# A feed-forward block with seven-product pairs: its start reordered, and one weight sum of each pair made by an accumulating DMA

## The chip, the cores and the metric

The kernel runs on one core of a Trainium2 chip. The metric is the device time of one execution in microseconds (us); lower is better. Everything below is read from one profiled execution of the kernel before the change.

## The reference, cut to what matters

The program computes two small transformer stacks for 256 tokens (two tiles of 128) of width 1024, all in 32-bit floats. The part that the change touches is the gated feed-forward of the first stack. It is computed four times: before and after the mixer, in each of two layers.

```python
D_MODEL, SEQ, D_FF = 1024, 256, 2816

def _swiglu(x, w1, w3, w2):
    return (jax.nn.silu(x @ w1) * (x @ w3)) @ w2

for l in range(DEPTH):                       # DEPTH = 2
    h = _swiglu(x, ffn_w1[l, 0], ffn_w3[l, 0], ffn_w2[l, 0])
    x = _layernorm(ALPHA * x + 0.5 * h, ln_g[l, 0], ln_b[l, 0])
    h = _mixer(x, l, ...)
    x = _layernorm(ALPHA * x + h, ln_g[l, 1], ln_b[l, 1])
    h = _swiglu(x, ffn_w1[l, 1], ffn_w3[l, 1], ffn_w2[l, 1])
    x = _layernorm(ALPHA * x + 0.5 * h, ln_g[l, 2], ln_b[l, 2])
# then the second stack (attention variants, squared-ReLU feed-forward), not touched
```

## The kernel before, in words

**Split products.** Every 32-bit product is made of three passes of a reduced form of float: a weight tile is split into a high part, which ScalarE writes by a cast (`w_high`), and a low part, which VectorE writes as raw minus high (`w_low`). TensorE then runs high by high, high by low and low by high. So each 1 MB weight unit (128 x 2048 values) costs ScalarE a cast, VectorE a subtraction, and TensorE 24 matmuls of 128 x 512 in a plain unit or 12 in a summed one.

**Ring of four slots.** The raw, high and low tiles have four slots. SyncE (SP) loads units in a fixed order; each load waits until VectorE has read the slot's former raw content (semaphore `slot_lo`). ScalarE waits until TensorE has used the slot's former high part (`unit_used`).

**One feed-forward.** The 2816 hidden columns are eleven blocks of 256. Five are plain (`h0`, `h1`, `h4`, `h7`, `h10`): two units each for the up products (`h1_0` is block 1, first half of K) and one for the down product (`d0`). The other six go in three pairs (`q` = 0, 1, 2) of the seven-product form, of which the kernel needs, for each pair, seven units made of four raw weight quarters R11, R21 (of w1), R12, R22 (of w3), each 128 x 2048. These stand in `sum_raw`, in the trace `buf_v` (R11), `buf_q` (R21), `buf_u` (R12) and `buf_val` (R22). The units are `b11` = R11 and `b21` = R21, then `v` = R11+R12, `x` = that plus R22, `w` = R12+R22, `y` = the sum in R11 plus R21, and `b22` = R22. `v`, `x` and `y` are made one after the other in the same tile R11, which can be overwritten only when the cast and the subtraction of the unit before have read it. `w` is made by an accumulating DMA that GpSimd issues (L705, semaphore `w_sum`); `v`, `x` and `y` are VectorE additions (`add_to`, L2671, semaphore `sum_done`). The left operands are four combinations of the quarters of x, the forms (`combine` L2704, cast to high L1974, low L2708), made once in each feed-forward.

**Order.** All engines run orders written out by hand, each in its own function: `ffn1` of SyncE, TensorE, ScalarE and VectorE. TensorE runs, in a pair, b11, b21, v, x, first half of a down product, w, second half, y, b22. Bank 1 of `aux` collects b11, then x, then w, then y, and ScalarE copies it out between them (`term1` after b11, `term2` after x, `term3` after w; L1997, L2006, L2010; `mix_param` in the trace). So TensorE starts `x` only after the term1 copy, `w` only after the term2 copy and `y` only after the term3 copy (semaphore `quad_act`).

**Start of a feed-forward.** TensorE runs block 0, block 1, the transposes of block 0's result (`plain_T(0)`), and then the down product d0, for which it needs the low part of that transposed result (`plain_low_T(0)`, L2681, `yT_low`). The down products collect in `acc`.

**End.** TensorE interleaves the last hidden block with the last down products (`last_T(t)` transposes block 10's result for token tile t; `last_low(t)`, L2694, is its low part); VectorE adds the result to x, takes the statistics and scales tile 0, then tile 1 (L2536 to L2585), while TensorE transposes the new x for the next stage (`x_T`, L842).

The cores of the functions follow, with the line numbers of the profile.

Of the kernel before, what the change touches and what calls it, by code (L numbers as in the profile page):

```python
# [48 lines left out]

def quad_and_plain(q, a, b):  # L50

    o = 3 * q + 4
    units = [(f"b11_{q}", a), (f"b21_{q}", b), (f"v_{q}", 1), (f"x_{q}", 2), (f"d{o - 3}", a), (f"w_{q}", b),
             (f"y_{q}", 1), (f"b22_{q}", 2), (f"h{o}_0", b), (f"h{o}_1", a), (f"d{o - 2}", 1), (f"d{o - 1}", 2)]
    done = [f"b11_{q}", f"b21_{q}", f"v_{q}", f"x_{q}", f"w_{q}", f"d{o - 3}", f"y_{q}", f"b22_{q}",
            f"h{o}_0", f"d{o - 2}", f"d{o - 1}"]
    return units, done


def ffn_units():  # L60

    order = [("h0_0", 0), ("h0_1", 1), ("h1_0", 3), ("h1_1", 1), ("d0", 2)]
    done = ["h0_0", "h1_0", "d0"]
    for q in range(QUADS):
        units, ends = quad_and_plain(q, *((3, 0) if q % 2 else (0, 3)))
        order += units
        done += ends
    order.append(("d10", 3))
    uses, loads, last_load, table = [0] * RING, [0] * RING, [None] * RING, {}
    for name, s in order:  # L70
        loaded = name[0] in "hd"
        table[name] = (s, uses[s], loads[s], last_load[s])
# [162 lines left out]
def build(nc, a, out, stop=None):  # L235
    ctx = ExitStack()
    with ctx:
# [67 lines left out]
        FORM_AT = (1, 2, 0, 3)  # L305
# [34 lines left out]
        w_sum = sem("w_sum")  # L340
        form_done = sem("form_done")
# [147 lines left out]
        def _(sp):  # L489
# [57 lines left out]
            def ffn1(l, which):  # L547
# [12 lines left out]
                for q in range(QUADS):  # L560
                    o = 3 * q + 4
                    down1(l, which, o - 3)
                    hidden1(l, which, o, 0)
                    down1(l, which, o - 2)
                    down1(l, which, o - 1)
# [90 lines left out]
        def _(pool):  # L656
# [42 lines left out]
            def sums_by_dma(l, which):  # L699

                for q in range(QUADS):
                    n = quads_before(l, which, q)
                    pool.wait_ge(sum_done, 3 * n + 1)
                    pool.wait_ge(r_full[R22], 16 * n + 16)
                    pool.dma_start(sum_raw[R12], sum_raw[R22], accum_op=ALU.add).then_inc(w_sum, 16)  # L705

# [98 lines left out]
        def _(pe):  # L805
# [196 lines left out]
            def ffn1(l, which, next_tile0):  # L1002
# [111 lines left out]
                def quad1(q):  # L1114
# [10 lines left out]
                    quad_product("x", q, 1, *form(1), False)  # L1125
                    plain_down(o - 3, 0)
                    pe.wait_ge(quad_act, terms + 2)
                    quad_product("w", q, 1, *form(2), False)
# [50 lines left out]
                quad_down(i - 2, 0)  # L1179
                quad_down(i - 1, 0)  # L1180
                last_T(0)
# [647 lines left out]
        def _(act):  # L1829
# [92 lines left out]
            def ffn1(l, which, tile1, next_tile0, mid):  # L1922
# [17 lines left out]
                def summed(q, n):  # L1940
                    act.wait_ge(sum_done, 3 * quads_before(l, which, q) + n)
# [24 lines left out]
                high_plain("h1_0")  # L1966
                high_plain("d0")
                activate(0, 1)
                high_plain("h1_1")
                loaded(0, R11)  # L1970
                high_sum("b11", 0, R11)
                for n in range(FORMS):
                    act.wait_ge(form_done, FORMS * (2 * l + which) + (1, 3, 2, 4)[n])
# [16 lines left out]
                for q in range(QUADS):  # L1990
# [11 lines left out]
                    summed(q, 3)  # L2002
# [15 lines left out]
                    high_plain(f"d{o - 2}")  # L2018
                    used(f"b22_{q}")
                    high_plain(f"d{o - 1}")  # L2020
# [6 lines left out]
                    high_sum("b11", q + 1, R11)  # L2027
                    activate(o, 1)
# [460 lines left out]
        def _(dve):  # L2489
# [165 lines left out]
            def ffn1(l, which, tile1, k_norm, next_tile0, mid, half_first):  # L2655
# [61 lines left out]
                multiply(0, 0)  # L2717
                whole(0, 0, 2)
                low_plain("h1_0")
# [5 lines left out]
                multiply(0, 1)  # L2725
                combine(2, 1, 2, ALU.subtract)
                dve.drain()
                combine(3, 3, 2, ALU.add)
                low_plain("h1_1")
# [4 lines left out]
                if mid is not None:  # L2734
                    mid()
                add_to(0, R11, R12)
                low_sum("b21", 0, R21)
                dve.wait_ge(aux_full[2], n_aux[2].k + 1)
                multiply(1, 0)
                plain_low_T(0)  # L2740
                multiply(1, 1)
                for q in range(QUADS):
# [7 lines left out]
                    add_to(q, R11, R21)  # L2750
# [13 lines left out]
                    low_plain(f"d{o - 2}")  # L2764
# [4 lines left out]
                    low_plain(f"d{o - 1}")  # L2769
                    multiply(o, 0)  # L2770
                    quad_low_T(q)
                    if q + 1 == QUADS:
                        break
                    low_sum("b11", q + 1, R11)
# [15 lines left out]
                if half_first:  # L2790
# [202 lines left out]
            def position_angles():  # L2993

                dve.wait_ge(angle_in, 2 * 16)
# [23 lines left out]
                dve.drain().then_inc(angles, 1)  # L3019
                dve.wait_ge(sines, 1)  # L3020
# [545 lines left out]
```

## Time and profile before

| what | value |
|---|---|
| median of 3 runs | 1984.37 us (1981.62 to 1985.58) |
| the profiled execution | 1983.09 us, its span 1981.1 us |
| TensorE busy | 1904.8 us, 96% of the span |
| VectorE busy | 1406.5 us, 71% |
| ScalarE busy | 1001.0 us, 51% |
| mean granted TensorE clock | 0.99 of full |
| the DMA engines, share of the span on the SP queue / GpSimd's queue | 48.9% / 6.0% |

The four feed-forwards of the first stack span about 0 to 212, 455 to 655, 655 to 850 and 1095 to 1300 us. TensorE is nearly always busy, so what counts is where it waits, and for what, and at which clock it runs behind the wait. A row of the timeline with "[6.08 <-DVE yT_low L2681]" says that the engine sat idle 6.08 us before this instruction and that VectorE's instruction of line 2681 ended the idle time. Durations of two instructions in a row overlap a little: subtractions of 2.28 us start 2.20 us apart.

### The profile page before, as it was taken

How to read it: one execution, taken by the hardware profiler on the slowest of the kernel's cores; microseconds unless marked ns; L12 is line 12 of the kernel's file. 1: busy time of each engine (PE TensorE's matmuls, PEld its weight loads, DVE VectorE, ACT ScalarE, POOL GpSimd, SP SyncE). 2: the span in 40 equal slices, each digit the busy share in tenths (PEclk: the TensorE clock that was granted, in tenths of full speed). 3: DMA queues.
4: the chain of work that ended last, by engine and by line, in shares of the span. 5: the costliest groups of instructions: out<-in, count | busy, mean ns of one | idle time of the engine just before them, and what ended most of it. 6: DMA issues, size and time to landing. Idle time of an engine off the chain costs nothing.

```text
span 1981.1 us, 23187 instructions
## 1 busy us (share of the span) xinstructions
PE 1904.8 (96%) x9016; PEld 1559.3 (79%) x9016; DVE 1406.5 (71%) x1599; ACT 1001.0 (51%) x1203; POOL 107.6 (5%) x176
## 2 busy tenths in 40 slices
PE   6999999999899899999999899989999999999999
PEld 5788788887788678878888678878788887778887
DVE  5788776678788878777667878778665567675545
ACT  4555435554455445543554455547654445654433
POOL 2001000000000000100000000011000000100000
PEclk9999999999999999999999999999999999999999
DMA  9665654456663666565345666456275545346552
GB/s 325 214 217 147 216 190 142 170 163 245 213 229 106 241 226 212 161 215 191 130 169 170 254 213 213 121 141 219 70 257 181 187 159 170 121 142 232 170 169 86
DMA packets 177729, 366.39 MB, mean 185 GB/s; under 512 B 7408, under 2 KB 51360, under 8 KB 176096
## 3 DMA queue, kind: packets, MB, share of 16 engines
q1 hardware_dynamic: 170512, 334.85, 48.9%
q0 software_dynamic: 7120, 30.21, 6.0%
q8 instruction: 66, 1.08, 0.2%
q14 instruction: 31, 0.25, 0.0%
HBM read 351.39 MB, written 1.05 MB: 178 GB/s over the span
## 4 chain that ended last, share of the span: by engine, by line
PE 83%; DVE 11%; ACT 3%; DVEq 1%; DMA 1%; issue 1%; SPq 0%; ACTq 0%
PE acc L827 51%; PE aux L827 15%; PE aux L1103 9%; DVE w_low L2497 4%; DVE buf_v L2671 1%; PE aux L842 1%; DVE w_low L2666 1%; DMA w_raw<-ffn_w 1%; ACT w_high L1935 1%; PE aux L938 1%; PE aux L1235 1%; DVE xT_low L2503 1%; PE aux L1066 1%; DVE form_low L2708 0%; DVE mix_param L2704 0%
## 5 line engine op out<-in xcount | busy, mean ns | idle before, releaser
L2497 DVE TENSOR_TENSOR w_low<-w_raw,w_high 128x2048 fp32r<-128x2048 f32 (+2 forms) x268 | 603.5, 2267 | 205.0 <-ACT w_high L1837 202.0
L1837 ACT CAST w_high<-w_raw 128x2048 fp32r<-128x2048 f32 (+2 forms) x268 | 503.3, 1893 | 257.7 <-PE acc L827 207.3
L827 PE MATMUL acc<-w_high,yT_high 128*128 128x512 f32 (+1 forms) x836 | 335.1, 401 | 31.0 <-DVE yT_low L2681 26.9
L827 PE MATMUL acc<-w_high,yT_low 128*128 128x512 f32 (+1 forms) x836 | 328.9, 393 | 0.0
L827 PE MATMUL acc<-w_low,yT_high 128*128 128x512 f32 (+1 forms) x836 | 328.8, 393 | 0.0
L827 PE MATMUL acc<-w_high,xT_high 128*128 128x512 f32 (+2 forms) x752 | 297.5, 396 | 5.1 <-DVE xT_low L2503 4.1
L827 PE MATMUL acc<-w_high,xT_low 128*128 128x512 f32 (+2 forms) x752 | 291.4, 388 | 0.0
L827 PE MATMUL acc<-w_low,xT_high 128*128 128x512 f32 (+2 forms) x752 | 291.1, 387 | 0.0
L827 PE MATMUL aux<-w_high,xT_high 128*128 128x512 f32 x576 | 230.7, 401 | 12.8 <-DVE w_low L2497 5.9
L827 PE MATMUL aux<-w_high,xT_low 128*128 128x512 f32 x576 | 225.8, 392 | 0.0
L827 PE MATMUL aux<-w_low,xT_high 128*128 128x512 f32 x576 | 225.3, 391 | 0.0
L827 PEld LDWEIGHTS acc<-w_high,yT_high 128*128 128x128 f32 x836 | 159.4, 191 | 67.8 <-issue 32.0
L827 PEld LDWEIGHTS acc<-w_high,yT_low 128*128 128x128 f32 x836 | 159.4, 191 | 33.8
L827 PEld LDWEIGHTS acc<-w_low,yT_high 128*128 128x128 f32 x836 | 159.8, 191 | 31.2
L827 PEld LDWEIGHTS acc<-w_high,xT_high 128*128 128x128 f32 x752 | 141.7, 188 | 37.5 <-DVE xT_low L2503 4.8
L827 PEld LDWEIGHTS acc<-w_high,xT_low 128*128 128x128 f32 x752 | 141.6, 188 | 28.8
L827 PEld LDWEIGHTS acc<-w_low,xT_high 128*128 128x128 f32 x752 | 141.8, 189 | 26.2
L1935 ACT CAST w_high<-buf_v 128x2048 fp32r<-128x2048 f32 x48 | 91.7, 1911 | 131.6 <-DVE buf_v L2671 88.7
L2666 DVE TENSOR_TENSOR w_low<-buf_v,w_high 128x2048 fp32r<-128x2048 f32 x48 | 109.9, 2289 | 59.0 <-ACT w_high L1935 59.0
L827 PEld LDWEIGHTS aux<-w_high,xT_high 128*128 128x128 f32 x576 | 108.9, 189 | 39.5 <-issue 8.9
L827 PEld LDWEIGHTS aux<-w_high,xT_low 128*128 128x128 f32 x576 | 108.7, 189 | 23.3
L827 PEld LDWEIGHTS aux<-w_low,xT_high 128*128 128x128 f32 x576 | 109.1, 189 | 21.0
(385 smaller groups left out, 2324.4 us busy)
## 6 DMA issues: line engine op xcount, KB each, us to landing
w_raw<-w_ff SPq DMA_DIRECT2D x64, 1024.0 KB
w_raw<-w_in SPq DMA_DIRECT2D x52, 1024.0 KB
w_raw<-ffn_w SPq DMA_DIRECT2D x44, 1024.0 KB
w_raw<-ffn_w SPq DMA_DIRECT2D x78, 512.0 KB
w_raw<-w_branch SPq DMA_DIRECT2D x16, 1024.0 KB
buf_v<-ffn_w SPq DMA_DIRECT2D x12, 1024.0 KB, 8.8
buf_u<-ffn_w SPq DMA_DIRECT2D x12, 1024.0 KB, 6.2
buf_q<-ffn_w SPq DMA_DIRECT2D x12, 1024.0 KB, 7.0
```

Source lines behind the costliest of these rows:

```text
L827: last = nc.tensor.matmul(dst, lhs[:, kt, tok], rhs(j), start=(kt == k_first and q == 0), stop=(kt == k_last and q == 2))
L842: last = nc.tensor.transpose(aux[:, b, k * P:(k + 1) * P], src[:, t, kt * P:(kt + 1) * P], ident[:])
L938: last = nc.tensor.transpose(aux[:, b, (2 * f + t) * P:(2 * f + t + 1) * P], gate_b[:, t, f0:f0 + P], ident[:])
L1066: last = nc.tensor.transpose(aux[:, b, (2 * f + t) * P:(2 * f + t + 1) * P], h[:, f0:f0 + P], ident[:])
L1103: last = nc.tensor.matmul(aux[:, b, :], lhs(k), rhs[:, s, k * NC:(k + 1) * NC], start=(first and k == 0 and n == 0), stop=(k == 3 and n == ...
L1235: last = nc.tensor.transpose(aux[0:width, b, (2 * k + t) * P:(2 * k + t + 1) * P], src(t, h), ident[:])
L1837: nc.scalar.copy(whi[:, s, 0:size], raw[:, s, 0:size]).then_inc(slot_hi[s], 1)
L1935: nc.scalar.copy(whi[:, s, :], sum_raw[r]).then_inc(slot_hi[s], 1)
L2497: V.tensor_tensor(wlo[:, s, 0:size], raw[:, s, 0:size], cast(whi[:, s, 0:size]), ALU.subtract)\
L2503: V.tensor_tensor(dst_l[:, k, tok], src, cast(dst_h[:, k, tok]), ALU.subtract)\
L2666: V.tensor_tensor(wlo[:, s, :], sum_raw[r], cast(whi[:, s, :]), ALU.subtract)\
L2671: V.tensor_tensor(sum_raw[r], sum_raw[r], sum_raw[other], ALU.add).then_inc(sum_done, 1)
```

## The change

**Slots (the table at the top).** `h1_1` moves from slot 1 to 2, `d0` from 2 to 1; in every pair `v` and `y` use slot 2 and `x` and `b22` slot 1 (before: 1 and 2). In the last pair the two late down products are loaded and split in the opposite order (`late_downs`), so `d8` stays in slot 1.

**Start of a feed-forward.** ScalarE casts h1_0, h1_1, waits for block 0's second tile, casts d0. VectorE makes the low part of h1_0 earlier, and does only the first of the four form low parts before `multiply(1, 0)` and `plain_low_T(0)`; the other three, the low part of b11, `multiply(1, 1)`, the sum for v and the low part of b21 come behind. The forms are made in another order, and v, x, w use the forms 0, 2, 1. The position angles of the second stack (`mid`, only in the first feed-forward) move from the start into the first two pairs.

**The sum for y.** VectorE's `add_to(q, R11, R21)` goes; GpSimd waits for the low part of x and issues an accumulating DMA R11 += R21; ScalarE waits for its semaphore `y_sum` before it casts y.

**End.** TensorE does `last_T(0)` one down half earlier. VectorE puts the low part of slot 0's next unit between the two passes of tile 0's scaling, and `last_low(1)` between its halves; the first half of tile 1's addition comes before the next stage's transposes in three of four cases (before: one), and in the mixer the second half comes before the low part of slot 3.

```diff
@@ quad_and_plain, ffn_units (slots)
+def late_downs(q):
+    downs = (f"d{3 * q + 2}", f"d{3 * q + 3}")
+    return downs if q + 1 < QUADS else downs[::-1]
-    units = [(f"b11_{q}", a), (f"b21_{q}", b), (f"v_{q}", 1), (f"x_{q}", 2), (f"d{o - 3}", a), (f"w_{q}", b),
-             (f"y_{q}", 1), (f"b22_{q}", 2), (f"h{o}_0", b), (f"h{o}_1", a), (f"d{o - 2}", 1), (f"d{o - 1}", 2)]
+    first, second = late_downs(q)
+    units = [(f"b11_{q}", a), (f"b21_{q}", b), (f"v_{q}", 2), (f"x_{q}", 1), (f"d{o - 3}", a), (f"w_{q}", b),
+             (f"y_{q}", 2), (f"b22_{q}", 1), (f"h{o}_0", b), (f"h{o}_1", a), (first, 2), (second, 1)]
-    order = [("h0_0", 0), ("h0_1", 1), ("h1_0", 3), ("h1_1", 1), ("d0", 2)]
+    order = [("h0_0", 0), ("h0_1", 1), ("h1_0", 3), ("h1_1", 2), ("d0", 1)]
@@ gpsimd, sums_by_dma
-                    pool.wait_ge(sum_done, 3 * n + 1)
+                    pool.wait_ge(sum_done, 2 * n + 1)
                     pool.wait_ge(r_full[R22], 16 * n + 16)
                     pool.dma_start(sum_raw[R12], sum_raw[R22], accum_op=ALU.add).then_inc(w_sum, 16)
+                    s, k = ffn_unit(l, which, f"x_{q}")
+                    pool.wait_ge(slot_lo[s], k + 2)
+                    pool.dma_start(sum_raw[R11], sum_raw[R21], accum_op=ALU.add).then_inc(y_sum, 16)
@@ tensor, quad1 and the end of ffn1
-                    quad_product("x", q, 1, *form(1), False)
+                    quad_product("x", q, 1, *form(2), False)
...
-                    quad_product("w", q, 1, *form(2), False)
+                    quad_product("w", q, 1, *form(1), False)
...
                 quad_down(i - 2, 0)
+                last_T(0)
                 quad_down(i - 1, 0)
-                last_T(0)
@@ scalar, ffn1
                 high_plain("h1_0")
+                high_plain("h1_1")
+                activate(0, 1)
                 high_plain("d0")
-                activate(0, 1)
-                high_plain("h1_1")
...
                     act.wait_ge(w_sum, 16 * quads_before(l, which, q) + 16)
                     high_sum("w", q, R12)
-                    summed(q, 3)
+                    act.wait_ge(y_sum, 16 * quads_before(l, which, q) + 16)
                     used(f"v_{q}")
                     high_sum("y", q, R11)
                     used(f"x_{q}")
                     nc.scalar.copy(term2, aux[:, 1, :]).then_inc(quad_act, 1)
@@ vector, ffn1
                 low_plain("d0")
-                low_sum("b11", 0, R11)
-                for n in range(FORMS):
-                    form_low(n)
-                if mid is not None:
-                    mid()
-                add_to(0, R11, R12)
-                low_sum("b21", 0, R21)
+                form_low(0)
                 dve.wait_ge(aux_full[2], n_aux[2].k + 1)
                 multiply(1, 0)
                 plain_low_T(0)
+                for n in range(1, FORMS):
+                    form_low(n)
+                low_sum("b11", 0, R11)
                 multiply(1, 1)
+                add_to(0, R11, R12)
+                low_sum("b21", 0, R21)
...
                     low_sum("x", q, R11)
                     low_plain(f"d{o - 3}")
-                    add_to(q, R11, R21)
                     low_sum("w", q, R12)
                     low_sum("y", q, R11)
@@ vector, end of ffn1 and mixer
-                tile_scale(l, k_norm, 0)
+                tile_scale(l, k_norm, 0, [0], between=lambda: low(0, ffn_n(l, which, 0) + FFN_USES[0]))
                 last_low(1)
-                low(0, ffn_n(l, which, 0) + FFN_USES[0])
+                tile_scale(l, k_norm, 0, [1])
-                if half_first:
+                if which == 0 or half_first:
                     add_first_half()
...
                 low(2, mixer_n(l, 2))
+                add_second_half(l)
                 low(3, mixer_n(l, 3))
-                add_first_half()
-                add_second_half(l)
```

**Where it moves instructions.** First VectorE at the start of the third feed-forward (layer 1, before the mixer). `buf_v` and `buf_q` are R11 and R21, `buf_k` the activation (`multiply`), L2708 (after: L2719) a form's low part, L2681 (L2692) the low part of the transposed result, L2671 (L2682) an addition. Before:

```order
L2497 TENSOR_TENSOR w_low<-w_raw,w_high 128x2048 x2
L2666 TENSOR_TENSOR w_low<-buf_v,w_high 128x2048
L2708 TENSOR_TENSOR form_low<-mix_param,form_high 128x512 x4
L2671 TENSOR_TENSOR buf_v<-buf_v,buf_u 128x2048
L2666 TENSOR_TENSOR w_low<-buf_q,w_high 128x2048
L2675 TENSOR_TENSOR buf_k<-buf_k,aux 128x256
L2681 TENSOR_TENSOR yT_low<-aux,yT_high 128x512
L2675 TENSOR_TENSOR buf_k<-buf_k,aux 128x256
L2666 TENSOR_TENSOR w_low<-buf_v,w_high 128x2048
L2681 TENSOR_TENSOR yT_low<-aux,yT_high 128x512
```

After:

```order
L2508 TENSOR_TENSOR w_low<-w_raw,w_high 128x2048
L2719 TENSOR_TENSOR form_low<-mix_param,form_high 128x512
L2686 TENSOR_TENSOR buf_k<-buf_k,aux 128x256
L2692 TENSOR_TENSOR yT_low<-aux,yT_high 128x512
L2719 TENSOR_TENSOR form_low<-mix_param,form_high 128x512 x3
L2677 TENSOR_TENSOR w_low<-buf_v,w_high 128x2048
L2686 TENSOR_TENSOR buf_k<-buf_k,aux 128x256
L2682 TENSOR_TENSOR buf_v<-buf_v,buf_u 128x2048
L2677 TENSOR_TENSOR w_low<-buf_q,w_high 128x2048
L2677 TENSOR_TENSOR w_low<-buf_v,w_high 128x2048
L2692 TENSOR_TENSOR yT_low<-aux,yT_high 128x512
```

The first `yT_low` now stands ahead of the low parts of b11 and b21, of three forms and of the addition for v. The second `yT_low`, which the addition for x follows, still stands behind all of them.

Then VectorE a little later, from the addition for x on, in the first pair. Before:

```order
L2671 TENSOR_TENSOR buf_v<-buf_v,buf_val 128x2048
L2666 TENSOR_TENSOR w_low<-buf_v,w_high 128x2048
L2497 TENSOR_TENSOR w_low<-w_raw,w_high 128x2048
L2671 TENSOR_TENSOR buf_v<-buf_v,buf_q 128x2048
L2666 TENSOR_TENSOR w_low<-buf_u,w_high 128x2048
L2666 TENSOR_TENSOR w_low<-buf_v,w_high 128x2048
```

After:

```order
L2682 TENSOR_TENSOR buf_v<-buf_v,buf_val 128x2048
L2677 TENSOR_TENSOR w_low<-buf_v,w_high 128x2048
L2508 TENSOR_TENSOR w_low<-w_raw,w_high 128x2048
L2677 TENSOR_TENSOR w_low<-buf_u,w_high 128x2048
L2677 TENSOR_TENSOR w_low<-buf_v,w_high 128x2048
```

One addition is gone. ScalarE's order inside a pair is the one that it had, but for its wait. Before, with the semaphores that each instruction waits for (the third row casts y, the fourth is the term2 copy):

```order
L1837 CAST w_high<-w_raw 128x2048 [waits slot_full0]
L1935 CAST w_high<-buf_u 128x2048 [waits w_sum,unit_used]
L1935 CAST w_high<-buf_v 128x2048 [waits unit_used,sum_done]
L2006 COPY mix_param<-aux 128x512 [waits unit_used]
L1935 CAST w_high<-buf_val 128x2048 [waits r_full3]
```

After:

```order
L1848 CAST w_high<-w_raw 128x2048 [waits slot_full0]
L1946 CAST w_high<-buf_u 128x2048 [waits w_sum,unit_used]
L1946 CAST w_high<-buf_v 128x2048 [waits unit_used,y_sum]
L2015 COPY mix_param<-aux 128x512 [waits unit_used]
L1946 CAST w_high<-buf_val 128x2048 [waits r_full3]
```

The cast of y now waits for the DMA, and the term2 copy still stands behind it.

## Rows read from the trace of the kernel before

**Rows 1.** The page: the chain that ended last, shares of the span by engine.
```profile
PE 83%; DVE 11%; ACT 3%; DVEq 1%; DMA 1%; issue 1%; SPq 0%; ACTq 0%
```

**Rows 2.** Waits of TensorE, whole span: in total, times, longest.
```profile
PE acc L827 <- DVE yT_low L2681: 26.9, 4, 8.6
PE aux L827 <- DVE buf_k L2675: 5.5, 1, 5.5
PE acc L827 <- DVE yT_low L2694: 3.7, 4, 0.9
```

**Rows 3.** Chain in order of time: start, length, what; 24 matmuls each.
```profile
99.63 5.44 PE acc L827 x24
...
694.62 8.53 PE acc L827 x24
...
1141.36 7.12 PE acc L827 x24
```

**Rows 4.** Windows: TensorE, its loads, VectorE, ScalarE, GpSimd busy; clock, DMA share, GB/s.
```profile
32.60:38.00 5.40, 5.31 (x13) 4.16 (x14) 5.31 (x5) 5.25 (x6) 0.00 (x0) 0.50 1.05 396
...
667.00:673.00 6.00, 5.20 (x27) 4.40 (x28) 4.08 (x7) 3.26 (x4) 1.16 (x2) 1.00 1.06 394
...
1303.00:1310.00 7.00, 5.98 (x27) 5.54 (x28) 6.04 (x10) 2.22 (x3) 1.66 (x2) 0.76 0.46 173
```

**Rows 5.** Timeline of VectorE, start of the third feed-forward: start, length, instruction.
```profile
671.72 1.29 DVE L2700 TENSOR_TENSOR mix_param<-xT_high,xT_low 128x512 f32<-128x512 f32 x2
...
688.95 2.29 DVE L2671 TENSOR_TENSOR buf_v<-buf_v,buf_u 128x2048 f32<-128x2048 f32 x1
...
704.30 0.69 DVE L2681 TENSOR_TENSOR yT_low<-aux,yT_high 128x512 fp32r<-128x512 f32 x1 [7.40 <-ACT yT_high L1950]
...
709.17 2.29 DVE L2666 TENSOR_TENSOR w_low<-buf_v,w_high 128x2048 fp32r<-128x2048 f32 x1 [1.98 <-ACT w_high L1935]
```

**Rows 6.** Timeline of TensorE there: first x product and first w product.
```profile
711.62 0.45 PE L1103 MATMUL aux<-w_high,form_high 128*128 128x512 f32 x1
...
718.43 0.50 PE L1103 MATMUL aux<-w_high,form_high 128*128 128x512 f32 x1 [1.13 <-ACT mix_param L2006]
```

**Rows 7.** Timeline of GpSimd: the accumulating DMA that makes w.
```profile
691.53 0.88 POOL L705 DMA_DIRECT2D buf_u<-buf_val  x1 [21.60 <-DVE buf_v L2671]
```

**Rows 8.** Line 705, issue to landing: all 12, then the one at 691.53.
```profile
DMA to landing us min/median/max: 6.9/7.0/10.1
...
DMA to landing us min/median/max: 10.1/10.1/10.1
```

**Rows 9.** The SP queue: packets, MB, share; windows 691 to 702 and 758 to 768.
```profile
q1 hardware_dynamic: 438, 1.64, 37.6%
...
q1 hardware_dynamic: 1302, 1.55, 53.9%
```

**Rows 10.** Second pair there: VectorE, ScalarE, TensorE, around w's first matmul.
```profile
755.93 2.29 DVE L2666 TENSOR_TENSOR w_low<-buf_v,w_high 128x2048 fp32r<-128x2048 f32 x1 [2.03 <-ACT w_high L1935]
...
760.43 2.29 DVE L2671 TENSOR_TENSOR buf_v<-buf_v,buf_q 128x2048 f32<-128x2048 f32 x1
...
762.76 1.92 ACT L1935 CAST w_high<-buf_v 128x2048 fp32r<-128x2048 f32 x1 [2.62 <-DVE buf_v L2671]
764.58 0.58 ACT L2006 COPY mix_param<-aux 128x512 f32<-128x512 f32 x1
...
766.18 0.39 PE L1103 MATMUL aux<-w_high,form_high 128*128 128x512 f32 x1
```

**Rows 11.** TensorE in the first feed-forward: first down product, first w product.
```profile
52.85 0.76 PE L827 MATMUL acc<-w_high,yT_high 128*128 128x512 f32 x1 [8.57 <-DVE yT_low L2681]
...
76.66 0.50 PE L1103 MATMUL aux<-w_high,form_high 128*128 128x512 f32 x1 [1.12 <-ACT mix_param L2006]
```

**Rows 12.** The first feed-forward's end: VectorE's low parts, TensorE's transposes.
```profile
213.94 6.68 DVE L2497 TENSOR_TENSOR w_low<-w_raw,w_high 128x2048 fp32r<-128x2048 f32 x3
...
226.38 1.27 PE L842 MATMUL aux<-ident,x_res 128*128 128x128 f32 x8 [1.53 <-issue]
```

More of the change, by code:

```diff
@@ L304, in build @@
         term1, term2, term3, silu1 = quarter
-        FORM_AT = (1, 2, 0, 3)
+        FORM_AT = (1, 0, 2, 3)
         R11, R21, R12, R22 = range(4)
@@ L340, in build @@
         w_sum = sem("w_sum")
+        y_sum = sem("y_sum")
         form_done = sem("form_done")
@@ L563, in ffn1 @@
                     hidden1(l, which, o, 0)
-                    down1(l, which, o - 2)
-                    down1(l, which, o - 1)
+                    for name in late_downs(q):
+                        down1(l, which, int(name[1:]))
                     hidden1(l, which, o, 1)
@@ L1940, in summed @@
                 def summed(q, n):
-                    act.wait_ge(sum_done, 3 * quads_before(l, which, q) + n)
+                    act.wait_ge(sum_done, 2 * quads_before(l, which, q) + n)
                 def activate(i, t):
@@ L1972, in ffn1 @@
                 for n in range(FORMS):
-                    act.wait_ge(form_done, FORMS * (2 * l + which) + (1, 3, 2, 4)[n])
+                    act.wait_ge(form_done, FORMS * (2 * l + which) + n + 1)
                     nc.scalar.copy(form_h[:, n, :, :].rearrange("p k c -> p (k c)"), quarter[FORM_AT[n]])\
                         .then_inc(form_hi, 1)
-                if mid is not None:
-                    mid()
                 used("h1_0")
@@ L2017, in ffn1 @@
                     nc.scalar.activation(silu1, aux[:, 1, :], ACT.Silu).then_inc(quad_act, 1)
-                    high_plain(f"d{o - 2}")
+                    high_plain(late_downs(q)[0])
                     used(f"b22_{q}")
-                    high_plain(f"d{o - 1}")
+                    high_plain(late_downs(q)[1])
                     activate(o, 0)
@@ L2027, in ffn1 @@
                     high_sum("b11", q + 1, R11)
+                    if mid is not None and q == 0:
+                        mid()
                     activate(o, 1)
@@ L2717, in ffn1 @@
                 multiply(0, 0)
+                low_plain("h1_0")
                 whole(0, 0, 2)
-                low_plain("h1_0")
                 whole(0, 1, 3)
@@ L2725, in ffn1 @@
                 multiply(0, 1)
+                low_plain("h1_1")
                 combine(2, 1, 2, ALU.subtract)
@@ L2728, in ffn1 @@
                 combine(3, 3, 2, ALU.add)
-                low_plain("h1_1")
                 low_plain("d0")
-                low_sum("b11", 0, R11)
-                for n in range(FORMS):
-                    form_low(n)
-                if mid is not None:
-                    mid()
-                add_to(0, R11, R12)
-                low_sum("b21", 0, R21)
+                form_low(0)
                 dve.wait_ge(aux_full[2], n_aux[2].k + 1)
@@ L2763, in ffn1 @@
                     V.tensor_tensor(term3, silu1, term3, ALU.mult).then_inc(h_ready, 1)
-                    low_plain(f"d{o - 2}")
+                    low_plain(late_downs(q)[0])
                     dve.wait_ge(unit_used, ffn_done(l, which, f"b22_{q}"))
@@ L2768, in ffn1 @@
                     V.tensor_tensor(term2, term1, term2, ALU.mult).then_inc(h_ready, 1)
-                    low_plain(f"d{o - 1}")
+                    low_plain(late_downs(q)[1])
                     multiply(o, 0)
@@ L2773, in ffn1 @@
                         break
+                    if mid is not None:
+                        mid(q)
                     low_sum("b11", q + 1, R11)
@@ L2992, in _, with position_angles @@
                 dve.sem_inc(s, 1)
-            def position_angles():
+            def position_angles(part):
+                if part == 1:
+                    return position_table()
                 dve.wait_ge(angle_in, 2 * 16)
@@ L3019, in position_angles, with position_table @@
                 dve.drain().then_inc(angles, 1)
+            def position_table():
                 dve.wait_ge(sines, 1)
```

## The prediction

> **What bounds the kernel now.** I read the chain that ended last first: TensorE makes 83% of it and VectorE 11% [rows 1], so a change pays only where it takes a wait away from TensorE, and costs only where it makes one. The waits of TensorE come next [rows 2]: the reader is to see that one line, the low part of block 0's transposed result, holds it four times, 26.9 us in all, and that another 5.5 us are lost once to an activation. Third, the chain in order of time [rows 3]: the same 24 matmuls that take 5.44 us inside a feed-forward take 8.53 us behind that wait, and 7.12 us in the fourth feed-forward. So a wait of 6 us costs 3.1 us (once 1.7) beside its own length. The windows say why: the granted clock is 0.50, which is 1.2 GHz, after the wait of 5.5 us; it stays at 1.00 (2.4 GHz) over a wait of 2.29 us in 667 to 673, and falls in 1303 to 1310 after one of 3.21 us [rows 4]. Last, the timelines of the start and of one pair [rows 5 to 7, 10].
>
> **The start of a feed-forward, third one.** The wait for `yT_low` is 6.1 us: the longest of the four is 8.6, which leaves 18.3 for the other three [rows 2]; here it ends at 694.62 [rows 3]. In the new order the first `yT_low` stands behind one form instead of behind b11, four forms, an addition and b21: three weight-sized instructions of 2.2 us and three forms of 0.6 us (an estimate from the 0.69 us of its tile-sized instruction, less overlap [rows 5]), 8.4 us, are taken out of its way. That is three times 2.2 and three times 0.6, and more than 6.1, so the wait goes, and with it 3.1 us of slow clock.
>
> What is late next is x. Its chain on VectorE holds the same instructions in both orders. Before, VectorE goes from 671.72 to the end of the low part of x at 709.17 + 2.29 = 711.46, 39.7 us, of which 7.40 us are idle before the second `yT_low` [rows 5]. That idle time came from TensorE's own wait and goes; 32.3 us of work and short waits stay, plus some 0.4 us that I give to the new places of the waits: x is ready at about 704.5. TensorE without its waits: it would have been at the down product at 694.6 - 6.1 = 688.5, and needs from there to x the 711.6 - 694.6 = 17.0 us [rows 3, 6] less 3.1 of slow clock, 13.9: it is due at x at 702.4. So 2.1 us of the wait come back in front of x, which begins at 704.6 instead of 711.62. Gain at this point: 7.0 us.
>
> **The sum for y.** The addition taken off VectorE (2.29 us at 760.43) is not on TensorE's path: w is multiplied at 766.18 without a wait [rows 10]. What replaces it is on it. ScalarE casts y and then copies term2, in this order, before and after; TensorE may not start w before that copy. Before, the copy starts at 764.58, 1.82 us after y's cast at 762.76, and w starts at 766.18. In the first pair of a feed-forward, where things are tighter, w follows the copy by 0.63 us, 6.81 us behind the start of x, after a wait of 1.13 us [rows 6].
>
> After the change, in the second pair: low part of x ends at 755.93 + 2.29 = 758.22. GpSimd issues 0.29 us later, as in 688.95 + 2.29 = 691.24 to 691.53 [rows 5, 7]. The DMA lands in 7.0 us at the median of 12, at least 6.9, at most 10.1 [rows 8]. Then 0.1 us to the cast of y, 1.82 to the copy, 0.63 to w: 758.22 + 0.29 + 7.0 + 2.55 = 768.06, a wait of 1.88 us if the DMA runs alone. It does not: behind the low part of the down unit, 2.2 us later, SyncE loads the next hidden unit (1 MB), and the SP queue moves 1.55 MB in 758 to 768. The one DMA of 10.1 us ran beside 1.64 MB of the SP queue [rows 9], 1.9 us more for each MB. About 0.75 MB of the load fall into the new DMA's time: 8.4 us. The wait is then 3.3 us. Two other weights are not at risk: y itself is cast in time, since it is due 5.4 us after w.
>
> Such a wait is as long as that of 3.21 us, behind which the clock fell. That window had a mean of 0.76 over 7 us, so 3.4 us at half speed, of which some 2.8 busy: 1.4 us lost. I take 3.3 + 1.4 = 4.7 us for each second and third pair. Everything behind w in the pair is tied to TensorE and moves with it. Eight pairs: -37.4 us. Bounds: 1.9 us each with the DMA alone at 7.0 and no fall of the clock (a wait of 2.29 kept it), 15 us; and at a landing of 10.1, 5.0 + 3.1 us each, 65 us.
>
> In the first pair, x begins when its low part ends, so w begins 0.13 + 7.0 + 1.4 + 2.55 = 11.1 us behind x, before 6.8: a loss of 4.3, and a wait of 5.7, behind which the clock surely falls, 2.8 us by rows 3. Sum of the third feed-forward's start: +7.0 - 4.3 - 2.8 = -0.1. The second is the same in the trace; the fourth has 1.4 less to win from the clock (7.12 against 8.53): -1.5. A slow clock behind the new wait at x costs nothing, since w waits for the DMA anyway.
>
> **The first feed-forward.** It has more to give: 8.57 us before the down product with 3.1 us of clock [rows 11], and 5.5 us before, because ScalarE waited for the data of d0 ahead of the activation; 13 matmuls run at half clock there [rows 4], at 0.43 instead of 0.23 us, 2.6 us. h1_1 in slot 2 is loaded without waiting, and the activation stands ahead of d0. I leave 0.3 us of the first wait and 1.0 of the second, since the loads are still short of time: 5.2 + 2.6 + 7.6 + 3.1 = 18.5, less some 3.4 us in front of x: +15.1 at x. Less 4.3 and 2.8: +8.0. The four starts together: +6.3.
>
> **The end.** `last_T(0)` one half of a down product (12 matmuls, 2.7 us) earlier takes away the four waits of 0.92 us [rows 2]: +3.7. In the mixer one low part (2.2 us) and the first half's addition leave the path of tile 1's scaling, which ends in the wait of 1.53 us at 226.38 [rows 12]; the other layer has the same place, so twice, less what stays: +2.8. The position angles leave the start of the first feed-forward, whose wait is 2.5 us longer than the others' [rows 2]; at their new place ScalarE's cast of the next pair's b11 hides them, since VectorE waits for it there: nothing; without that cover 2.5 once. A low part inside tile 0's scaling is hidden by TensorE's remaining down products; if it is not, it can cost up to its 2.2 us in each.
>
> **Sum.** +6.3 - 37.4 + 6.5 = -24.6 us: 1983.1 of the profiled execution becomes 2007.7. That execution was 1.3 us below the median of the three runs, which I add: 2009 us, slower by 1.2%.
>
> **What a page says against it.** The rows say 7.0 us for a DMA of 1 MB from GpSimd that accumulates [rows 8]. The Trainium skill, "DMA: Bandwidth & Descriptors", section "Anatomy of one DMA — SWDGE (gpsimd) path", fits 2.0 us plus the bytes over 436 GB/s, an estimate of 4.4 us for 1 MB; that fit is not for accumulation. By it, y's sum would land 2.6 us sooner than by the rows and w would start in time. The trace disagrees with it by 2.6 us in its best case, and the sum goes by the trace.
>
> **The rivals.**
> (1) The DMA's landing is near its 7.0 us and the clock mostly holds. For it: most of the twelve landed so. Against it: they ran mostly beside an idle SP queue, and this one will not. Eight pairs cost 15 us; a first pair loses 2.9 us and 1.7 of clock, so the starts give 15.1 - 4.6 + 2 x (7.0 - 4.6) + (7.0 - 1.4 - 4.6) = 16.3; the end 6.5. Net +7.8: 1977 us, faster. It decides below a wait of about 2.3 us, that is a landing under 7.4 us.
> (2) The wait never shows at w: the sum lands before ScalarE would need it (a landing under 5.1 us). Then the starts give all, 15.1 + 7.0 + 7.0 + 5.6 and 1.1 each, 39, and the end 6.5: 1939 us. Against it: no DMA of the twelve was under 6.9.
> (3) Heavy sharing: a landing of 9.5 to 10 us, as in the one case beside full SP traffic. Wait 4.6, clock 2.5: eight pairs 57 us, first pairs lose 5.4 + 3.0: starts +1.1; net -49: 2034 us.
> (4) The start does not get faster by the 7 us at x, since VectorE's backlog is longer than I reckon: 3 us more in each, 12 us on top of the forecast: 2021 us.
>
> **How the numbers follow.** Forecast 0.52, with a range of its own from 1996 to 2022; (1) 0.16; (2) 0.05; (3) 0.13; (4) 0.09; the rest, 0.05, lies at no change between (1) and the forecast. A measurement of this kernel can tell about 0.2%, 4 us, from no change. Faster: (2) and most of (1), 0.18; same: 0.06; slower: 0.76. The range of 1980 to 2030 leaves out (2), some of (1) and the upper part of (3).
>
> **What would show it.** The waits of TensorE should name the term2 copy (before L2006) twelve times, some 5.7 us in the first pairs and 3.3 in the others, where it had 1.1 us in the first pairs alone; ScalarE idle before y's cast, ended by a DMA; line `yT_low` of block 0 gone from TensorE's waits; a wait of 2 to 3 us for a low part before the first x of each feed-forward; granted clock at one half for a few us behind most of w's starts. A landing near 7 us beside the SP load would make the forecast wrong by 11 us and more; if w starts without a wait in the second and third pairs, its main term is wrong.

## The result: 1.0% slower, and the profile after

The changed kernel takes 2004.36 us at the median of four runs (1995.68 to 2012.12), the kernel before 1983.46 (1981.62 to 1985.58). The ratio is 1.0104, with a 95% interval of 1.0052 to 1.0155: slower, by about 21 us. The profiled execution took 1998.71 us, with a span of 1996.9 and a mean granted clock of 0.988 (before: 0.990).

The page first: the chain that ended last, by engine and then the head of the list by line.

```profile
PE 70%; DVE 13%; DMA 6%; ACT 5%; issue 4%; DVEq 1%; POOL 0%; SPq 0%; POOLq 0%; ACTq 0%
```

TensorE had 83% of the chain and the DMAs 1% [rows 1]. It now has 70%, and the DMAs 6%. The waits of TensorE say where they came in; each row has the total, the times and the longest.

```profile
PE aux L1114 <- ACT mix_param L2015: 39.0, 12, 5.2
PE aux L1114 <- DVE w_low L2677: 9.9, 4, 2.7
...
PE acc L838 <- DVE yT_low L2692: 3.0, 1, 3.0
```

The wait of 26.9 us for `yT_low` has shrunk to one of 3.0, and the single wait of 5.5 us and the four of 0.9 us are gone [rows 2]. In their place are twelve waits for the copy of term2 (L2015), 39.0 us, one in each seven-product pair, and four for the low part of x, 9.9 us. The timeline of TensorE in the third feed-forward has them in place: x and w of the first pair, then w of the second and of the third.

```profile
708.83 0.76 PE L1114 MATMUL aux<-w_high,form_high 128*128 128x512 f32 x1 [2.65 <-DVE w_low L2677]
...
719.72 0.80 PE L1114 MATMUL aux<-w_high,form_high 128*128 128x512 f32 x1 [3.64 <-ACT mix_param L2015]
...
773.42 0.67 PE L1114 MATMUL aux<-w_high,form_high 128*128 128x512 f32 x1 [2.90 <-ACT mix_param L2015]
...
825.74 0.50 PE L1114 MATMUL aux<-w_high,form_high 128*128 128x512 f32 x1 [2.75 <-ACT mix_param L2015]
```

x began at 711.62 and w at 718.43 [rows 6]. This feed-forward already starts 4.47 us late, because the ones ahead of it lost time, so x at 708.83 is 7.3 us gained within it, and w at 719.72 is 3.2 gained.

The copy itself takes 0.58 us. What it stands behind is seen in the second pair: the low part of x on VectorE, the DMA on GpSimd, then ScalarE.

```profile
760.10 2.29 DVE L2677 TENSOR_TENSOR w_low<-buf_v,w_high 128x2048 fp32r<-128x2048 f32 x1 [2.03 <-ACT w_high L1946]
...
762.69 0.85 POOL L716 DMA_DIRECT2D buf_v<-buf_q  x1 [11.89 <-DVE w_low L2677]
...
770.98 1.90 ACT L1946 CAST w_high<-buf_v 128x2048 fp32r<-128x2048 f32 x1 [6.67 <-DMA buf_v<-buf_q]
772.79 0.58 ACT L2015 COPY mix_param<-aux 128x512 f32<-128x512 f32 x1
```

The low part ends at 762.39, GpSimd issues 0.30 us later, the sum is there at 770.98, ScalarE casts it and only then copies term2, at 772.79; w starts at 773.42. ScalarE idles 6.67 us, where it idled 2.62 for VectorE's addition [rows 10]. What the cast (L1946) waited for this DMA in all, and the twelve landings, from the view of the line that issues it:

```profile
  ACT w_high L1946: 80.5, 12
...
DMA to landing us min/median/max: 8.1/8.3/8.5
```

The load beside it (queue q1, packets, MB and share of the DMA engines), while this DMA was on its way, 762.69 to 770.96:

```profile
q1 hardware_dynamic: 276, 0.28, 9.8%
```

In the same window of the other eleven it is 0.26 to 0.29 MB, and 0.36 MB for the one of 8.5 us.

### The profile page after: what moved, and what is told of

Its sections match the earlier page's. It is cut to its first block, busy times and chain, and to the rows that moved or that the text cites. A ratio compares the mean times of both kernels' runs of the same rounds, so it can differ in the third digit from the quotient of the medians.

```text
span 1996.9 us, 23187 instructions
## 1 busy us (share of the span) xinstructions
PE 1914.0 (96%) x9016; PEld 1563.6 (78%) x9016; DVE 1382.2 (69%) x1587; ACT 1000.7 (50%) x1203; POOL 120.4 (6%) x188
## 4 chain that ended last, share of the span: by engine, by line
PE 70%; DVE 13%; DMA 6%; ACT 5%; issue 4%; DVEq 1%; POOL 0%; SPq 0%; POOLq 0%; ACTq 0%
PE acc L838 43%; PE aux L838 15%; PE aux L1114 5%; DMA buf_v<-buf_q 5%; DVE w_low L2677 4%; ACT w_high L1946 3%; DVE w_low L2508 2%; DVE buf_v L2682 2%; PE aux L853 1%; DMA buf_q<-ffn_w 1%; PE aux L949 1%; PE aux L1246 1%; DVEq L2560 1%; DVE xT_low L2514 1%; DVE yT_low L2692 0%
## 5 line engine op out<-in xcount | busy, mean ns | idle before, releaser
L1946 ACT CAST w_high<-buf_v 128x2048 fp32r<-128x2048 f32 x48 | 91.6, 1908 | 201.8 <-DMA buf_v<-buf_q 80.5
L1114 PE MATMUL aux<-w_high,form_high 128*128 128x512 f32 x192 | 83.1, 433 | 48.9 <-ACT mix_param L2015 39.0
```

The costliest lines, as they stand in the source:

```text
L1114: last = nc.tensor.matmul(aux[:, b, :], lhs(k), rhs[:, s, k * NC:(k + 1) * NC], start=(first and k == 0 and n == 0), stop=(k == 3 and n == ...
L1946: nc.scalar.copy(whi[:, s, :], sum_raw[r]).then_inc(slot_hi[s], 1)
```

## The experiments

Each kernel was timed beside the kernel before, which had medians of 1982.93 us (first four experiments) and 1983.35 (last four). The diffs leave out the counts of `sum_done` that go with an addition more or less.

**1. y's sum back on VectorE, all the rest of the change kept.**

```diff
-                    s, k = ffn_unit(l, which, f"x_{q}")
-                    pool.wait_ge(slot_lo[s], k + 2)
-                    pool.dma_start(sum_raw[R11], sum_raw[R21], accum_op=ALU.add).then_inc(y_sum, 16)
...
-                    act.wait_ge(y_sum, 16 * quads_before(l, which, q) + 16)
+                    summed(q, 3)
                     used(f"v_{q}")
...
+                    add_to(q, R11, R21)
```

> The change with the sum for y put back on VectorE (an addition behind the low part of the down unit), everything else as changed. Theory (the new DMA delays y's cast, the term2 copy stands behind that cast, and w waits for the copy): all twelve waits before w go, but for some 1.1 us in each first pair. The starts then give what they gave at the first x product in the changed kernel, 12.8 + 7.3 + 7.3 + 5.9 = 33 us, less up to 1.7 us of slow clock behind three of the waits at x, and the ends 6 us: about 34 us under the kernel before, 1949 us. Rival (the reordered start or end is what costs, or VectorE's spare time is what the change needs): no faster than the kernel before, 1985 to 2000 us.

Measured: 1948.03 us (1947.04 to 1951.07), ratio 0.9824 (0.9808 to 0.9840). Against the whole change's 1.0104, the DMA costs 2.8% or 56 us; all other edits together gain 35. (By the starting times in the changed kernel's profile, x is 12.8, 6.6, 7.3 and 5.2 us sooner in the four feed-forwards; the expectation has 7.3 and 5.9 for the second and the fourth.) The waits of TensorE for x stay (11.7 us), and those for the term2 copy shrink to one:

```profile
PE aux L1111 <- DVE w_low L2674: 11.7, 4, 3.6
...
PE aux L1111 <- ACT mix_param L2012: 1.1, 1, 1.1
```

**2. The converse: the kernel before, with nothing but y's sum by DMA.**

```diff
+                    s, k = ffn_unit(l, which, f"x_{q}")
+                    pool.wait_ge(slot_lo[s], k + 2)
+                    pool.dma_start(sum_raw[R11], sum_raw[R21], accum_op=ALU.add).then_inc(y_sum, 16)
...
-                    summed(q, 3)
+                    act.wait_ge(y_sum, 16 * quads_before(l, which, q) + 16)
...
-                    add_to(q, R11, R21)
```

> The kernel before with one edit: the sum for y by the accumulating DMA. Theory: w waits 3.0 us in each second and third pair, 1.0 us of slow clock on top on average, 8 x 4 = 32 us; in the first pairs w comes 4.2 us later and the clock falls for 2.8 us, 4 x 7 = 28 us; about 2043 us. Rival (the DMA is harmless without the new order of the start): within 5 us of the kernel before.

Measured: 2047.41 us (2045.92 to 2049.78), ratio 1.0326 (1.0309 to 1.0343): 64 us for the one edit. Its waits of TensorE:

```profile
PE aux L1107 <- ACT mix_param L2010: 43.4, 12, 5.2
PE acc L831 <- DVE yT_low L2685: 28.0, 4, 9.6
```

The old wait for `yT_low` is still there, so its removal is the work of the new order and not of a relieved VectorE. The waits for the copy are 43.4 us, where the kernel before had 4.5, so 39 are new. The rest of the 64 fits the slower clock: a mean of 0.976 over 2044.5 us against 0.990 over 1981.1 is 29 us more at full speed lost, an estimate, of which some falls into the waits themselves.

**3. The changed kernel, with the term2 copy ahead of the wait for the sum.** The same instructions, two of them in the other order on ScalarE.

```diff
-                    act.wait_ge(y_sum, 16 * quads_before(l, which, q) + 16)
-                    used(f"v_{q}")
-                    high_sum("y", q, R11)
                     used(f"x_{q}")
                     nc.scalar.copy(term2, aux[:, 1, :]).then_inc(quad_act, 1)
+                    act.wait_ge(y_sum, 16 * quads_before(l, which, q) + 16)
+                    high_sum("y", q, R11)
```

> The changed kernel with ScalarE's term2 copy moved ahead of its wait for the DMA and of y's cast. The DMA, its length and VectorE's work stay. Theory (it is the place in ScalarE's queue, not the DMA's length in itself): w no longer waits; y is cast some 0.4 us before it is due in second and third pairs and 1.8 us late in first pairs; 1949 + 7 = about 1956 us. Rival (the DMA is too long wherever it stands): the wait moves to y with most of its length, 3 us in each pair, and the time stays near 2000 us.

Measured: 1959.00 us (1955.78 to 1959.45), ratio 0.9872 (0.9855 to 0.9888). The DMAs are as slow as they were, as the line that issues them shows:

```profile
DMA to landing us min/median/max: 8.1/8.3/10.0
```

and yet 45 us are back, and no wait for the copy is left in the view of TensorE's waits:

```profile
PE aux L1114 <- DVE w_low L2676: 13.1, 7, 3.5
...
PE aux L1114 <- DVE mix_param L2766: 1.6, 5, 0.3
```

So most of the loss was not that y is late. It was that the wait for y stood ahead of something that TensorE needed sooner. Against experiment 1, 11 us remain; experiment 7 gets back 7 of them.

**4. The changed kernel, with SyncE holding the next hidden unit's load until the sum has landed.**

```diff
                         down1(l, which, int(name[1:]))
+                    sp.wait_ge(y_sum, 16 * quads_before(l, which, q) + 16)
                     hidden1(l, which, o, 1)
```

> The changed kernel with one more wait on SyncE: the load of the next hidden unit's second half is issued only when the DMA of y's sum has landed. Theory (the DMA takes 8.3 us instead of 7.0 because it shares the DMA engines with that load): landing 7.0 us in all twelve, the waits before w 1.3 us shorter, 12 x 1.3 = 16 us, and most falls of the clock behind them gone, 3 to 10 us: 1978 to 1987 us. Rival (a DMA whose source and sum were written a moment ago takes 8.3 us by itself): landing stays at 8.3 us, time near 2004 us or above, since the load comes later.

Measured: 1988.12 us (eight runs, 1980.39 to 1993.18), ratio 1.0024 (1.0010 to 1.0038), just above the expected band. The landings, and the waits of TensorE:

```profile
DMA to landing us min/median/max: 6.9/6.9/9.1
```

```profile
PE aux L1115 <- ACT mix_param L2016: 25.8, 12, 3.7
PE aux L1115 <- DVE w_low L2678: 11.5, 4, 3.5
```

Without the load beside it the sum lands 1.4 us sooner at the median, and the waits are 13.2 us shorter in all (39.0 to 25.8). That the load is what makes the landing 8.3 us is shown. The falls of the clock did not get fewer, as the expectation had it: the mean clock is 0.987, against 0.988. Two landings took 9.1 us, in the second pairs of the second and the fourth feed-forward, and brought the two longest waits, 3.73 us at 566.84 and 3.74 at 1212.04. The clock behind the first:

```profile
566.00:573.00 7.00, 6.16 (x15) 4.82 (x16) 5.20 (x4) 3.22 (x5) 0.00 (x0) 0.51 1.04 367
```

No load ran beside those two. What the view of the DMA queues has in each of their windows, beside the sum itself, is one packet of the queue that it calls "instruction":

```profile
q8 instruction: 1, 0.02, 0.6%
```

Of the twelve landings here, the four with such a packet took 7.6, 9.1, 7.6 and 9.1 us, and the eight without one 6.9 to 7.0. In experiment 7, with the load held as well, seven have one and took 6.9 to 9.1, and the five without took 6.9 to 7.0. That the packet is the cause isn't shown.

**5. Experiment 1, with VectorE's addition for x ahead of a transposed low part**, in every pair, so that x is ready sooner.

```diff
-                    plain_low_T(1 if q == 0 else o - 3)
                     add_to(q, R11, R22)
+                    plain_low_T(1 if q == 0 else o - 3)
                     low_sum("x", q, R11)
```

> The first experiment's kernel (sum for y on VectorE) with the low part of the second transposed result moved behind the addition for x, where VectorE idles 1.98 us for ScalarE. Theory (x is late because of VectorE's backlog of the start): x is ready 0.6 us sooner, its wait in the first pairs 2.65 becomes 2.05 us, 4 x 0.6 = 2.4 us and perhaps a fall of the clock less: 1944 to 1946 us. Rival (x waits for something else, ScalarE or the forms): wait stays 2.65 us, 1948 us.

Measured: 1944.88 us (1943.58 to 1945.64), ratio 0.9805 (0.9792 to 0.9819). The wait for x falls from 11.7 to 9.3 us, which is the gain expected of it:

```profile
PE aux L1111 <- DVE w_low L2674: 9.3, 4, 2.9
```

**6. Experiment 1 without the edits at the feed-forward's end and in the mixer.** `last_T(0)`, the low part inside tile 0's scaling and the first half's addition stand where they stood before:

```diff
-                last_T(0)
                 quad_down(i - 1, 0)
+                last_T(0)
...
-                tile_scale(l, k_norm, 0, [0], between=lambda: low(0, ffn_n(l, which, 0) + FFN_USES[0]))
+                tile_scale(l, k_norm, 0)
                 last_low(1)
-                tile_scale(l, k_norm, 0, [1])
+                low(0, ffn_n(l, which, 0) + FFN_USES[0])
...
-                if which == 0 or half_first:
+                if half_first:
                     add_first_half()
...
-                add_second_half(l)
                 low(3, mixer_n(l, 3))
+                add_first_half()
+                add_second_half(l)
```

> The first experiment's kernel with the edits at the end of the feed-forward and in the mixer undone (order of last_T(0), tile scaling, halves of the addition, low part of slot 3). Theory: the ends gave 6.1 us in the changed kernel's profile, so 1948 + 6 = 1954 us, with the four waits of 0.92 us before the last down product back. Rival (the ends are hidden by the next stage): 1948 us.

Measured: 1954.15 us (1953.41 to 1954.22), ratio 0.9854 (0.9839 to 0.9869). The end's edits are worth 6.1 us; the old waits are back:

```profile
PE acc L835 <- DVE yT_low L2702: 3.7, 4, 0.9
PE aux L850 <- issue: 2.8, 2, 1.5
```

**7. Experiments 3 and 4 together: the copy first, and the load held.**

```diff
+                    sp.wait_ge(y_sum, 16 * quads_before(l, which, q) + 16)
...
-                    act.wait_ge(y_sum, 16 * quads_before(l, which, q) + 16)
-                    used(f"v_{q}")
-                    high_sum("y", q, R11)
                     used(f"x_{q}")
                     nc.scalar.copy(term2, aux[:, 1, :]).then_inc(quad_act, 1)
+                    act.wait_ge(y_sum, 16 * quads_before(l, which, q) + 16)
+                    high_sum("y", q, R11)
```

> The changed kernel with both repairs: the term2 copy ahead of y's cast, and the load held until the DMA has landed. Theory (both effects, place in the queue and shared DMA engines, make the whole loss): landing 7.0 us, y is cast in time in second and third pairs and at most 0.5 us late in first ones: 1948 to 1953 us, the time of the first experiment. Rival (taking 2.3 us of addition off VectorE in each pair is worth something by itself once the DMA is harmless): under 1944 us.

Measured: 1951.77 us (1950.16 to 1952.88), ratio 0.9844 (0.9828 to 0.9859). This is the DMA at its best here, and its median is still 3.7 us above that of experiment 1, where VectorE makes the sum; the single runs overlap (1950.16 at the lowest here, 1951.07 at the highest there), so the two may be equal. It does take twelve additions off VectorE. The pages of experiment 1 and of this one show TensorE equally busy, and VectorE 31 us less:

```profile
PE 1898.8 (98%) x9016; PEld 1555.7 (80%) x9016; DVE 1405.7 (72%) x1599; ACT 1000.8 (51%) x1203; POOL 110.3 (6%) x176
```

```profile
PE 1898.8 (97%) x9016; PEld 1552.1 (80%) x9016; DVE 1374.8 (71%) x1587; ACT 999.6 (51%) x1203; POOL 120.2 (6%) x188
```

The relief gained nothing that the latency didn't take back.

**8. Experiment 5 with the copy ahead of y's cast**, the sum on VectorE: both good orders in one.

```diff
-                    summed(q, 3)
-                    used(f"v_{q}")
-                    high_sum("y", q, R11)
                     used(f"x_{q}")
                     nc.scalar.copy(term2, aux[:, 1, :]).then_inc(quad_act, 1)
+                    summed(q, 3)
+                    high_sum("y", q, R11)
```

> The kernel of the sooner x sum with the term2 copy ahead of y's cast as well, the sum for y on VectorE. Theory: the wait of 1.1 us before w in each first pair, for the same copy behind the same cast, goes too: 4 us under that kernel, 1940 to 1942 us. Rival (another wait takes its place, since the low part of y comes later): 1944 to 1948 us.

Measured: 1944.53 us (1944.04 to 1945.27), ratio 0.9805 (0.9792 to 0.9819): no gain over experiment 5, where 1940 to 1942 was expected. There were only two waits for the copy to win in experiment 5, 2.2 us in all, not four. They are gone, but w now waits for its own low part, twice. In the second feed-forward, TensorE's first w product:

```profile
501.38 0.47 PE L1111 MATMUL aux<-w_high,form_high 128*128 128x512 f32 x1 [0.96 <-DVE w_low L2673]
```

and VectorE ahead of it, the addition for y and then w's low part, back to back behind x's low part (492.26) and a down unit's (494.54):

```profile
492.26 2.29 DVE L2673 TENSOR_TENSOR w_low<-buf_v,w_high 128x2048 fp32r<-128x2048 f32 x1 [1.38 <-ACT w_high L1943]
494.54 2.29 DVE L2504 TENSOR_TENSOR w_low<-w_raw,w_high 128x2048 fp32r<-128x2048 f32 x1
496.75 2.28 DVE L2678 TENSOR_TENSOR buf_v<-buf_v,buf_q 128x2048 f32<-128x2048 f32 x1
498.95 2.28 DVE L2673 TENSOR_TENSOR w_low<-buf_u,w_high 128x2048 fp32r<-128x2048 f32 x1
```

w's low part ends at 498.95 + 2.28 = 501.23, and w starts 0.15 us later. Experiment 5 has these four at the same times within 0.03 us, and there w starts at 501.88 without a wait: a fall of the clock behind x (mean 0.68 in 494.7 to 500) had made TensorE itself later. The fourth feed-forward is the place where only the copy differs. Experiment 5, and then this one:

```profile
1127.36 0.50 PE L1111 MATMUL aux<-w_high,form_high 128*128 128x512 f32 x1 [1.09 <-ACT mix_param L2012]
```

```profile
1127.07 0.47 PE L1111 MATMUL aux<-w_high,form_high 128*128 128x512 f32 x1 [0.99 <-DVE w_low L2673]
```

In experiment 5 the copy ends at 1127.31 and w's low part at 1127.08, so the copy ahead could win 0.2 us and no more. The view of TensorE's waits has six for low parts, 11.3 us in all, against four of 9.3 us in experiment 5. On VectorE, y's addition stands ahead of w's low part; putting it behind would be the thing to try, and wasn't tried.

## Why the prediction was right in its mechanism, and where its sizes were off

Forecast 2009 us, measured 2004.36: 4.6 less. The mechanism held in its main steps: twelve waits named by the term2 copy, ScalarE idle before y's cast until a DMA ends, `yT_low` gone from the waits of the later feed-forwards, a wait of 2.65 us before their first x. Of the signs that the prediction names, one failed: the clock was to fall behind most of w's starts, and fell behind six of twelve.

**The landing.** Predicted 8.4 us, from 7.0 alone and 1.9 for each MB beside it; measured 8.3 at the median. Experiment 4 confirms the first half, 6.9 without the load, and that the load makes the rest. How the rest was made up is wrong twice, and that it came out is luck: 0.28 MB of the load fell into the DMA's time, not 0.75, and they cost 1.3 us, which is 4.7 for each MB and not 1.9. The Trainium skill, "DMA: Bandwidth & Descriptors", section "Anatomy of one DMA — SWDGE (gpsimd) path", would make the landing 4.4 us, an estimate by its fit; the section doesn't say whether the fit holds for an accumulating transfer. This one took 6.9 us even undisturbed, 2.5 more (the prediction's 2.6 goes with the median of 7.0, not with its best case).

**The second and third pairs: predicted -37.4, measured -28.7.** I take the starting time of the same instructions in both traces. The shift grows by 7.9 us over these pairs in the first feed-forward, 6.5 in the second, 7.9 in the third and 6.3 in the fourth. The wait was sized at 3.3 us and is 2.9 on average: the twelve sum to 39.0, the four of the first pairs (5.16, 3.63, 3.64, 3.58) to 16.0, which leaves 23.0 for eight, 3.4 less than forecast. The larger miss is the slow clock behind them, sized at 1.4 us each. It fell behind two of the eight. Windows of the profile after, of the pair at 773 and the next one at 825; the column ahead of the last two is the clock:

```profile
773.00:780.00 7.00, 6.58 (x22) 5.26 (x23) 5.78 (x4) 4.10 (x4) 0.00 (x0) 0.76 0.94 319
825.50:832.00 6.50, 6.26 (x28) 5.18 (x29) 6.29 (x5) 5.20 (x6) 0.00 (x0) 1.00 0.00 2
```

The waits are 2.90 and 2.75 us, and one of 3.19 in the second feed-forward had no fall behind it either. Two falls at 1.8 us are 3.6 us, where I had 11.2. Waits and falls make 26.6 of the 28.7. The other 2.1, a quarter of a microsecond in each pair, is in how a wait is counted: products in a row start 0.23 us apart and last 0.39, so that a wait, which is counted from the end of the one before, delays the next start by its length and 0.16 us; and the first product behind it takes 0.50 us instead of 0.39. The prediction left both out. My step was: "Such a wait is as long as that of 3.21 us, behind which the clock fell." One row had been made a rule for eight places. The length of a wait doesn't decide it: in experiment 7 the clock stayed at 1.00 behind a wait of 3.51 us at 56.88, and in experiment 5 it fell behind one of 2.04 at 494.72. That this term differs between executions is likely: the four runs were 1995.68 and 1998.71 us at clocks of 0.989 and 0.988, and 2010.0 and 2012.12 at 0.983 and 0.982. Only one of them has a profile, so in which pairs the clock fell in the others stays open. It would also explain why the median lies 5.7 us above the profiled execution.

**The starts: predicted +6.3, measured +7.2.** By feed-forward the forecast was +8.0, -0.1, -0.1 and -1.5; it came out as +5.95, +1.2, +0.3 and -0.25. The gain of 7.0 us at x in the third was 7.3. Three sizes were off. In the first feed-forward a wait for `yT_low` of 2.98 us stands where I left 1.0:

```profile
39.13 0.47 PE L838 MATMUL acc<-w_high,yT_high 128*128 128x512 f32 x1 [2.98 <-DVE yT_low L2692]
```

There x came 12.8 us sooner, not 15.1, and w 8.7 (67.92 against the 76.66 of [rows 11]). Behind w the slow clock was to cost 2.8 us in each; it did in the first and the third, and cost 1.3 and 1.4 in the second and the fourth, which is why these two came out better. And the wait at w in the other first pairs is 3.6 us, not 5.7 (5.4 by the prediction's own terms, 11.1 less 6.8 plus the 1.13 that it had): the clock falls behind the wait at x, so that the products between x and w run slowly while the DMA is on its way, and use up part of what would have been a wait. I had written that this slow clock costs nothing, but hadn't taken it off the wait. The sum isn't touched by that, since w came 4.1 us later against x, where I had 4.3.

**The end: predicted +6.5, measured +6.1** in the trace, and 6.1 again by experiment 6. The wait of 1.53 us [rows 12] is gone; the same transposes after:

```profile
226.66 1.04 PE L853 MATMUL aux<-ident,x_res 128*128 128x128 f32 x8
```

**The sum.** +7.2 - 28.7 + 6.1 is -15.4, beside +15.8 us of span. Of the forecast's error of 4.6 us, the pairs are +8.7, the starts +0.9 and the end -0.4 in the profiled execution, 9.2 together. The median of the runs lies 5.7 us above that execution, where I had added 1.3, which takes 4.4 of it back. That half of the error in the profiled execution vanishes in the median is luck: nothing in the prediction says that the new kernel's time would spread by 16 us.

**The rivals.** The first (a landing near 7 us and a clock that mostly holds, 1977 us) is half of what experiment 4 sets up: there the landing is 6.9, and the time 1988, since the twelve waits are still 2.15 us on average and the clock, 0.987, didn't hold. The second (the wait never shows, 1939 us) needs a landing that no run has; but experiments 1 and 5, which take the wait away by other means, are at 1948 and 1945. The other two didn't occur.

## What to carry to other kernels

Here an addition moved from an engine with slack to a DMA gained nothing and added latency: 2.3 us of work became 8.3 us of waiting. Before putting a wait on an engine that works in order, look at what stands behind it in the queue and who needs that: one copy moved ahead of the wait gave back 45 of the 56 us. Undo each half of a mixed change before judging it, since here the halves had opposite signs: the new orders alone are 35 us faster, and with x's sum one step sooner 38.5.

## What the runs showed of the hardware

An accumulating DMA of 1 MB between two buffers of the chip, issued by GpSimd, takes 6.9 to 7.0 us from issue to landing alone, and in the changed kernel 8.1 to 8.5 with the first 0.26 to 0.36 MB of a load on SyncE's queue beside it. With the load held, it took up to 9.1 when one 16 KB packet of the "instruction" queue ran beside it, and never more than 7.0 without one (experiments 4 and 7); in experiment 3, with 0.90 MB of loads and such a packet beside it, one took 10.0. The cause of the 9.1 us isn't shown. In the changed kernel TensorE's clock falls to half behind some waits of 2.65 to 2.98 us and stays up behind others of 2.75 to 3.19, and the same kernel then takes 1996 or 2012 us. The runs of each kernel without these waits lie within 4.1 us (experiments 1, 5, 6 and 8), but so do those of experiment 2, which has twelve of them, so the waits alone don't make the spread.
